# A hybrid transformer layer pair on one core: one plain gate unit per merge instead of two, and a new order of products in the first block-product unit

## The reference, cut to what matters

```
# first block, three branches (y_a, y_b, y_c of width 512)
gates  = sigmoid(h @ w_in[:, gate columns] + b_gate)          # 3 x 1024 columns
merged = gates[0] * (y_a @ wa) + gates[1] * (y_b @ wb) + gates[2] * (y_c @ wc)
# second block, two branches
gate_a, gate_b = sigmoid(h @ w_in_2[...]), sigmoid(h @ w_in_2[...])   # 2 x 1024 columns
merged = gate_a * (attn @ w_proj_attn) + gate_b * (sgu @ w_proj_sgu)
```

## Time and profile before

| | |
|---|---|
| median of 3 runs | 3371.44 us (3370.37 to 3371.47) |
| the profiled execution's own time | 3371.2 us |
| its span, first to last instruction | 3369.4 us |
| TensorE busy | 3272.0 us, 97% |
| VectorE busy | 2046.8 us, 61% |
| ScalarE busy | 1256.1 us, 37% |
| GpSimd busy | 1198.9 us, 36% |
| mean granted TensorE clock | 0.994 |

### The profile page before, as it was taken

The page is one execution under the profiler, slowest core; times in us unless marked ns, Lnnn a source line. Parts: engine busy times, 40 slices in busy tenths (PEclk is TensorE's granted clock), DMA queues, the critical chain, the costliest instruction groups (busy, mean ns, idle before and its releaser), DMA issues.

```text
span 3369.4 us, 41098 instructions
## 1 busy us (share of the span) xinstructions
PE 3272.0 (97%) x16387; PEld 2697.9 (80%) x16387; DVE 2046.8 (61%) x2805; ACT 1256.1 (37%) x2008; POOL 1198.9 (36%) x495
## 2 busy tenths in 40 slices
PE   7999999999999999999899999999999999999998
PEld 6788877888888888787678888888788888888786
DVE  6883446542647766999743344445644376666789
ACT  4233444333236454334533333333332252333333
POOL 2442101544313444545212222222443144454453
PEclk9999999999999999999999999999999999999999
DMA  4233102335523444544221212213235233333543
GB/s 132 62 85 98 32 21 81 106 106 185 183 95 138 168 164 167 191 155 157 87 86 50 62 56 56 63 58 95 106 125 192 96 113 112 110 112 117 212 153 109
DMA packets 240745, 378.75 MB, mean 112 GB/s; under 512 B 22136, under 2 KB 180516, under 8 KB 227756
## 3 DMA queue, kind: packets, MB, share of 16 engines
q1 hardware_dynamic: 210172, 255.58, 23.7%
q10 hardware_dynamic: 26000, 109.81, 8.3%
q0 software_dynamic: 4384, 10.74, 0.9%
HBM read 263.66 MB, written 110.33 MB: 111 GB/s over the span
## 4 chain that ended last, share of the span: by engine, by line
PE 81%; DVE 10%; DMA 2%; issue 2%; ACT 2%; POOL 2%; ACTq 0%; SPq 0%; DVEq 0%; POOLq 0%
PE ps L1306 28%; PE ps L350 17%; PE ps L2088 7%; PE ps L831 5%; PE ps L305 3%; PE ps L1461 2%; PE ps L1463 2%; PE ps L1452 2%; PE ps L3754 2%; PE ps L3725 1%; PE ps L367 1%; PE ps L3237 1%; PE ps L3742 1%; PE ps L326 1%; PE ps L333 1%
## 5 line engine op out<-in xcount | busy, mean ns | idle before, releaser
L297 POOL TENSOR_TENSOR wlo<-raw,whi 128x2048 fp32r<-128x2048 f32 (+1 forms) x85 | 298.8, 3515 | 839.0 <-ACT whi L289 838.6
L1306 PE MATMUL ps<-h_hi,own 128*128 128x512 f32 x1200 | 385.6, 389 | 0.0
L1306 PE MATMUL ps<-tb,whi 128*128 128x512 f32 x1200 | 370.9, 390 | 3.3 <-POOL wlo L1014 3.3
L350 PE MATMUL ps<-h_lo,whi 128*128 128x512 f32 x880 | 351.8, 400 | 0.7 <-POOL wlo L297 0.7
L350 PE MATMUL ps<-h_hi,wlo 128*128 128x512 f32 x880 | 344.4, 391 | 0.0
L986 POOL TENSOR_TENSOR own<-raw,own 128x1024 fp32r<-128x1024 f32 x50 | 142.0, 2841 | 468.5 <-ACT own L976 468.5
L2088 PE MATMUL ps<-dw,h_lo 128*128 128x512 f32 x1152 | 271.2, 395 | 16.2 <-DVE big L1957 8.7
L2088 PEld LDWEIGHTS ps<-dw,h_lo 128*128 128x128 f32 x1152 | 218.5, 191 | 66.3 <-issue 19.5
L1306 PEld LDWEIGHTS ps<-tb,whi 128*128 128x128 f32 x1200 | 225.8, 188 | 51.1 <-POOL wlo L1014 4.1
L1306 PEld LDWEIGHTS ps<-h_hi,own 128*128 128x128 f32 x1200 | 225.2, 188 | 46.7
L1014 POOL TENSOR_TENSOR wlo<-wsum,whi 128x2048 fp32r<-128x2048 f32 x50 | 238.3, 4766 | 61.5 <-ACT whi L1009 61.5
(11 more groups left out here) (417 smaller groups left out, 7515.0 us busy)
## 6 DMA issues: line engine op xcount, KB each, us to landing
raw<-in_w_ff_dram SPq DMA_DIRECT2D x32, 1024.0 KB, 5.5
raw<-in_w_in_dram SPq DMA_DIRECT2D x57, 512.0 KB, 4.6
raw<-in_w_in_dram SPq DMA_DIRECT2D x28, 1024.0 KB, 5.4
f_keep<-fr ACTq DMA_DIRECT2D x27, 1024.0 KB, 3.9
s_keep<-fr ACTq DMA_DIRECT2D x24, 1024.0 KB, 5.2
xh<-s_keep SPq DMA_DIRECT2D x48, 512.0 KB, 3.7
g_keep<-fr ACTq DMA_DIRECT2D x20, 1024.0 KB, 3.9
fr<-g_keep SPq DMA_DIRECT2D x20, 1024.0 KB, 4.9
```

The source lines that it names most:

```text
L297: nc.gpsimd.tensor_tensor(wlo[c % 2][:, 0:cols], raw[c % 2][:, 0:cols], whi[c % 2][:, 0:cols].bitcast(F32), ALU.subtract).then_inc(s_lo.se ...
L350: x = nc.tensor.matmul(ps[:, bank, :], w(a, k, m * P, P), H[b][:, k, sl], start=j == 0, stop=j == 23)
L1306: last = nc.tensor.matmul(ps[:, bank, :], w[p][:, k, :], x[r][:, k, :], start=k == 0 and q == 0, stop=k == 3 and q == 2)
```

## The change

Merges get PLAIN = 1 (the feed-forward stages keep 2). Unit 1 becomes a block-product unit whose order is A11, A12, S4, S2, S1, S3, A22. The wait for the unit's weight-sum parts stands at every S product and the one for the own parts at every A product, instead of both at the first. VectorE makes unit 1's weight sums ahead of all token sums; ScalarE makes the high part of those sums ahead of T1's and T2's. GpSimd's split_lo of unit 1 goes; pool_ups splits the own parts and the sums of unit 1 in its place. The first bank's wait for an earlier plain unit is left out where there is none.

```diff
--- before.py
+++ after.py
@@ -911,6 +911,8 @@
 
             def order(self, i):
 
+                if self.PLAIN == 1 and i == 1:
+                    return "A11", "A12", "S4", "S2", "S1", "S3", "A22"
                 return ("S2", "S1", "S3", "A22", "A11", "S4", "A12") if i == self.nu - 1 else (
                     "S2", "S1", "S3", "A11", "S4", "A12", "A22")
 
@@ -1135,11 +1137,14 @@
                     if i < plain:
                         if i:
                             self.keep(e, i - 1)
+                        if plain == 1:
+                            prepare_sums(1)
                         if i == self.first:
                             self.token_hi(e, "T1", "T2")
                         for k, x in enumerate(self.PLAIN_ORDER):
                             if k == 1:
-                                prepare_sums(i + 1)
+                                if plain > 1:
+                                    prepare_sums(i + 1)
                                 if i == self.first:
                                     self.token_hi(e, "T3")
                             if self.is_gate(i):
@@ -1230,13 +1235,15 @@
                     times(i, {"C22": 0, "C12": 1, "C11": 2, "C21": 3}[x], x, dst)
 
                 for i in range(self.first, plain):
+                    if plain == 1:
+                        self.weight_sums(e, 1)
                     if i == self.first:
                         self.token_sums(e, *self.steps[:-2])
                     for k, x in enumerate(self.PLAIN_ORDER):
                         if not self.is_gate(i):
                             e.wait_ge(pe_a.sem, self.a + 4 * i + k + 1)
                             times(i, k, x, ps[:, 4 * (i % 2) + k, :])
-                        if i + 1 == plain and k == 0:
+                        if i + 1 == plain and k == 0 and plain > 1:
                             self.weight_sums(e, plain)
                         if i == self.first and k == 0:
                             self.token_sums(e, "T3")
@@ -1285,10 +1292,11 @@
                     c = self.u + i
                     for k_th, a in enumerate(self.order(i)):
                         bank, n_th = self.bank_of(i, a), 7 * (i - plain) + k_th
-                        if k_th == 0:
+                        if a[0] == "S":
                             e.wait_ge(s_lo.sem, c + 1)
+                        else:
                             e.wait_ge(own_lo.sem, self.ol + i - plain + 1)
-                        if n_th in (0, 4):
+                        if n_th in (0, 4) and plain - 2 + n_th // 4 >= 0:
                             self.taken(e, plain - 2 + n_th // 4)
                         elif n_th >= 8:
                             self.after_product(e, n_th - 8)
@@ -1320,7 +1328,7 @@
         class Merge(Seven):
 
 
-            def __init__(self, w_in, gate_col, w_branch, bias, banks_free=None, plain=2):
+            def __init__(self, w_in, gate_col, w_branch, bias, banks_free=None, plain=1):
                 super().__init__()
                 self.banks_free = banks_free
                 self.w_in, self.gate_col, self.wb, self.bias = w_in, gate_col, w_branch, bias
@@ -1402,7 +1410,6 @@
                         self.y_split_hi(e, j // 4 + 1)
 
             def pool(self, e):
-                split_lo(e, self.up(1))
                 self.pool_ups(e)
                 split_lo(e, self.branch_unit(0), 4 * 256)
                 self.y_split_lo(e, 0)
```

## The result

The changed kernel takes 3387.05 us (median of 6 runs, 3384.53 to 3389.09) against 3371.45 for the kernel before beside it: ratio 1.0047, 95% interval 1.0037 to 1.0057. It is 15.6 us slower, with less matmul work.

What follows compares the result with a forecast made beforehand. TensorE was taken as the bound, busy 3272.0 of 3369.4 us. Each merge loses 6.7 us plus 1.2 of clock, 15.8 in all on 3371.2: 3387.0, or 3387.2 as median; range 3380.5 to 3392.

Steps and rivals of the forecast that it cites:

- The saving: In each merge a 21.8 us plain unit becomes a 19.04 us product unit: 2.72 us, 5.4 over both.
- Head of the chain: First merge, VectorE and GpSimd: unit 1's sums and splits make the chain 6.2 us later; T3's low part ends at 596.6.
- S2: Unit 1's product S2 waits for T2's low part: 1.1 us in the first merge, 6.3 in the second.
- A22: Unit 1's seventh product waits 6.5 us for T4's low part in each merge.
- Unit 2: The next unit's first product waits another 1.7 us for the low part of its sums, in both merges.
- Clock: TensorE's slow clock after long waits costs 1.2 us per merge, bounds 0 and 3.5.
- The stronger form: TensorE's clock: a full slow stretch follows each long wait, 1.8 us per merge, total 17.0 instead of 15.8.
- Sum: Whole kernel: 6.7 + 6.7 + 1.2 + 1.2 = 15.8 us slower, 3387.2 us as median.
- Signs: TensorE's waits for VectorE's low parts: 7 to 8 us, then about 13; third unit ends 6.7 to 8.5 later per merge.
- (a): Rival, both merges: the clock costs 2 to 3.5 us per merge, 3389 to 3392; chance 0.12 for over 3390.
- (b): Rival, both merges: splits fit beside VectorE, chain up to 7.4 us shorter, 3371 to 3380; chance 0.06.
- (c): Rival: not slower, the three products cover everything in both merges, 3364; chance 0.04, 0.03 more for within 0.2%.

Runs made afterwards that it cites:

- x9: Changed kernel with unit 1's sums made before the stage's waits, its low parts on VectorE, T4's high part earlier, unit 2 also A11 first: 3363.16 us, 0.9982 of kernel before.
- x5: Changed kernel with unit 1's low parts (own blocks and sums) made by VectorE instead of GpSimd: merges gain 2.7 and 3.5 us, the total 7.6.
- x3: Changed kernel with the old order S2, S1, S3, A11, S4, A12, A22 in the first product unit: merges 3.0 and 1.9 us longer.
- x7: Changed kernel with ScalarE making T4's high part ahead of unit 2's own parts: merges 2.6 and 2.7 us longer.
- x1: Kernel before with the change in the first merge alone: that merge 240.5 us, unchanged second merge 167.8, total some 17 us above the kernel before.
- x4: Kernel before, two plain units, with the new order in the first product unit of each merge: ratio 1.0004.
- x4b: Two plain units with the new order once more, for a second profile: ratio 1.0003.

## Why the prediction was right, and where it was not

**Sign, size and mechanism** were right: 3387.2 forecast, 3387.05 measured. By steps:

- *The saving.* 12 matmuls a merge, 2.7 us. x9 shows it bare: 2.7 us in the first merge.
- *Head of the chain.* T3's low part was put 33.3 us after VectorE's entry; 32.9 measured. The three splits of GpSimd in the chain are shown by x5.
- *S2.* Forecast waits 1.1 and 6.3, measured 0.89 and 7.93. The second is larger because VectorE entered 9.5 us late, not 7.5: a term that the prediction took from the earlier trace rows and that moved by 2.0. The prediction gave no reason why it should stay.
- *A22.* Forecast 6.5 in both; measured 6.04 and 4.25. The second is smaller because S2, S1 and S3 ran 2.1 us slower after the long wait and ended later.
- *Unit 2.* A wait of 1.7 was forecast in both; none is in the trace. Its time is there, inside A22, which took 4.42 us (609.94 to 614.36) instead of 2.72.
- *Clock.* This term was mis-sized. The granted clock in the 5 us windows around A22 of the first merge:

```profile
605.00:610.00 5.00, 0.06 (x1) 0.09 (x1) 5.00 (x3) 3.21 (x4) 4.11 (x3) 0.65 0.06 26
610.00:615.00 5.00, 5.00 (x15) 3.90 (x16) 3.99 (x7) 2.06 (x4) 4.23 (x1) 0.66 0.01 3
```

  The slow stretch came, on A22, but nearly all of its 1.7 us lie in the time in which unit 2 would have waited for its split: unit 2 began 0.1 us after that split had ended and took 19.10 us, and 19.18 in the second merge, against 19.04. So the clock cost some 0.1 to 0.2 us per merge, not 1.2. The stronger form, by which each long wait is followed by a full slow stretch at 1.2 GHz, is borne out as to the clock (0.53 in the 5 us from 2405 and 0.74 in those from 2420, at the two long waits of the second merge) and wrong as to the cost.
- *Sum.* The merges lost 6.4 and 8.3 us, 14.7 in all, against 7.9 + 7.9 forecast; 0.3 us came from the rest of the profiled span, 15.0 together. That the total fits to 0.2 us is partly luck: the clock was put some 2 us too high, the late entry 2 us too low and the chain in both merges together some 0.9 too long, and the median lies 0.8 above the profiled execution's 3386.28.
- *Signs.* TensorE's waits for low parts were 6.9 and 12.2 us, about as said, and the third unit ended 6.4 and 8.3 us later, the first just outside the 6.7 to 8.5 named. In (a) the sum's upper end should read 20.4 (13.4 and twice 3.5), not 21.

**The rivals.** (b), splits that delay the chain less, is excluded by x5 and by the 2.77 us rows. (c) needed T4 at A22's turn, 38.2 us after the merge's start. In x9's first merge its low part ends after 37.0 and A22 does not wait, so the point was right; x9 made four changes to reach it, and whether fewer do was not tried. The prediction's view that the order is "enough there" for S2 was right within 0.9 us in the first merge, and x3 shows how little that was worth. (a) is excluded: the median stayed under 3390, and the clock cost less than forecast.

## What to carry to other kernels

When a covering stretch is cut, add up the whole queue of the engine behind it, with every instruction that excludes it on a shared resource: the wait to expect is at the last operand that queue delivers, not at the first. A reordering that hides the first wait pays only as far as the last one leaves room, and moving work from GpSimd to a busy VectorE can shorten both. If several waits are in a row, the slow clock behind an earlier one can vanish in the next (the changed kernel) and is paid in full behind the last (x3, x7: 1.8 to 2.8 us). And when an edit saves a few microseconds, compare the stage's time in the profile and not only the total: here the stages outside the merges, which no edit was meant to change, moved by 12 us.

## What was not expected

The last down projection has a wait of 4 us in the profiles of x1, x4 and x4b and in none of the other eleven; a GpSimd split that gets in ahead of a VectorE sum is what the rows show, and its cause is open. With what follows, it takes back all that x4 gains. The store that opens the second merge lands 2 us later in every changed kernel than in both profiles of the kernel before, so part of the second merge's loss is not the covering unit's. The change also adds waits to each product of the feed-forward stages, and the page counts 298 more instructions; whether that moved either was not tried.
